# First norm's squares on ScalarE, the bias copy in eight requests, and idle products before the first chunk: one change to a hybrid decoder layer on Trainium2

## The chip, the core and the metric

The kernel runs on one core of one Trainium2 chip. The metric is the device time of one launch in microseconds (us); lower is better. The core has TensorE (PE, with its weight loads in a row of their own, PEld), VectorE (DVE), ScalarE (ACT), GpSimd (POOL), SyncE (SP), and sixteen DMA engines that all queues share. All inputs and outputs are in device memory.

## The reference, cut to what matters

One decoder layer is computed for a prompt of 256 tokens and for eight samples of four tokens (288 token columns in all, D = 2048), with the same weights:

```
mod = silu(c) @ w_ada + b_ada                 # 9 condition rows, 2048 x 12288 weights
shift1, scale1, gate1, shift2, scale2, gate2 = split(mod, 6)
h = rmsnorm(x, norm1_g) * (1 + scale1) + shift1
qa, ka, va, qb, kb, vb, r, glr = split(h @ w_in)
oa = dilated attention(qa, ka, va, rel_bias)  # 16 heads, prompt and samples
ob = gated linear attention(qb, kb, vb, gates from glr)   # 4 heads
x = x + gate1 * (concat(norm(oa), norm(ob) * silu(r)) @ w_out)
h2 = rmsnorm(x, norm2_g) * (1 + scale2) + shift2
x = x + gate2 * conv_ffn(h2)                  # w_up 2048 x 11264, w_down 5632 x 2048
```

`rmsnorm(x, g)` is `x * rsqrt(mean(x*x) + EPS) * g`, in float32. The prompt's attention adds to each score a bias that depends on the distance of query and key alone; it comes from a table of 32 buckets per head.

## The kernel before, in words

Everything is float32. A large product is made of three passes on TensorE with weights and activations split in an upper and a lower part (`three`, L903 to L905). Weights come in slabs of 1 MB into a ring of four slots; ScalarE makes the upper part of a chunk (L1418, 128 x 1024), VectorE the lower part (L1920), and TensorE multiplies: 24 matmuls a chunk. The 96 chunks of `w_in` are numbered j; a loop over j on every engine sets the order by hand, and the work of the other stages is woven into it at fixed numbers: slabs of `w_ada` (four matmuls, each in a quarter of the array, L853), the four heads of the linear attention (`head`, j from 28 on, eight apart) and the eight pairs of attention heads (`pair`, j from 63 on, four apart). Then follow the samples' attention, the output projection, the second norm and the two halves of the FFN.

The places that the change touches:

- **Start.** TensorE first runs six products that nobody reads (L796, 128 x 256), then turns x from rows of tokens to columns (`x_turns`, L818, 48 transposes), together with the condition rows and some vectors. VectorE copies each turned tile to `xT` (L1765).
- **First norm.** ScalarE squares `xT` in four pieces of 128 x 1152 (`norm_square`, L1367). TensorE sums each piece over the partitions by a product with ones (`norm_sum`, L839), which puts the sum of a token into all 128 partitions; a piece is woven between two slabs of `w_ada` (`early_slab`, L853). VectorE makes the mean (L1827), ScalarE takes logarithm and exponential (L1377, L1379), each after a load of its table, and VectorE multiplies `xT` by the root (`norm_rooted`, L1841).
- **Condition.** Slabs 0 to 7 of `w_ada` give the first group of shift and scale. After slab 3 and after slab 7 ScalarE copies the result rows (`ada_rows`, L1437), TensorE turns them (`early_turn`, L860, with nine columns), VectorE adds the bias (L1822), and modulates (L1897 to L1905). Only then can the first chunk be multiplied.
- **Bias.** A table of 16 x 512 is written to `bias_rows` in device memory (L699). One request (L706) copies it to `bias_full`, [16 heads, 128, 256], each row shifted by one element against the row before: 2048 pieces of 1 KB, device memory to device memory. GpSimd waits for it at once, and loads the first states of the linear attention (L715) after that. In the stage of the pairs, GpSimd loads the bias of each pair of heads from `bias_full` (L732, 256 KB). Its loop over the pairs is a hardware loop of four rounds.
- **Queues.** SP issues the slabs of `w_in` and the first ones of `w_ada` (L517, L539), ACT the later ones of `w_ada` (`lead_load`, L1455, and `late_load`, L1462); each waits until a slot is free. What GpSimd issues stands in a queue of its own.

Of the kernel before, what the change touches and what calls it, by code (L numbers as in the profile page):

```python
# [14 lines left out]
P = 128  # L15
# [119 lines left out]
def build(nc, a, o, bias_rows, bias_full):  # L135
    ctx = ExitStack()
    with ctx:
# [65 lines left out]
        rel_rows = projf[:, 11328:11456]  # L203
        sq = projf[:, 11520:13824].rearrange("p (j n c) -> p j n c", j=2, n=4)
        sq2 = [work[:, t:t + 2 * TOK].rearrange("p (n c) -> p n c", n=2) for t in (0, 944)]
# [32 lines left out]
        def old_state(b):  # L238
# [80 lines left out]
        PA_ = st("prep_scalar", "silu_c")  # L319
        NT = [st("norm1_tensor", "s0", "s1", "s2", "s3"), st("norm2_tensor", *(f"s{n}" for n in range(8)))]  # L320
        NA = [st("norm1_scalar", "q0", "q1", "q2", "q3", "ln", "rs"),
              st("norm2_scalar", *(f"q{n}" for n in range(8)), "ln", "rs")]
        NM = [st(f"norm{n}_mean", "ms") for n in (1, 2)]

# [186 lines left out]
        def _(sp):  # L511
            def ada_load(s):

                i, at = s // 8, 512 * (s // 8) + D * (s // 4 % 2)
                place, slot, _ = ada_home(s)
                dst = slab(slot, 4, 512) if place == 0 else (first_rows, lead_rows)[place - 1][slot]
                sp.dma_start(dst, w_ada[:, 4 * (s % 4):4 * (s % 4) + 4, at:at + 512]  # L517
                             ).then_inc((full, first_in, lead_in)[place][slot], 16)
# [57 lines left out]
            for s in range(2):  # L576
                sp.wait_ge(raw_used, s + 3)
                ada_load(s + 8)
            sp.wait_ge(*PT_.upto("x15"))
            ada_load(10)  # L580
            sp.wait_ge(*NT[0].upto("s3"))
            ada_load(11)
# [95 lines left out]
        def _(pool):  # L678
# [25 lines left out]
            pool.dma_start(wg2, a["w_gate2"][0]).then_inc(wg2_in, 16)  # L704
            slant = bass.AP(bias_rows[:, :].tensor, P - 1, [[512, H_A], [-1, P], [1, SEQ]])
            pool.dma_start(bias_full[:, :, :], slant).then_inc(slant_out, 16)  # L706
            pool.wait_ge(slant_out, 16)

            s_in = a["state_gla"][0].rearrange("(s e) h k v -> k h e s v", e=2)
            s_out = o["new_gla_s"].rearrange("(s e) h k v -> k h e s v", e=2)  # L710
            for h in range(H_B):
                if h:
                    pool.wait_ge(s0_out, 32 * h)
                for e in range(2):
                    pool.dma_start(s0[:, :, e, :], s_in[:, h, e]).then_inc(s0_in, 16)  # L715
                pool.wait_ge(*RA.upto("stp", h))
                pool.dma_start(o["new_gla_p"][h], stp).then_inc(stp_out, 16)
                pool.wait_ge(*RV.upto("state1", h))
                for e in range(2):
                    pool.dma_start(s_out[:, h, e], s0[:, :, e, :]).then_inc(s0_out, 16)  # L720

            pool.wait_ge(*RN.upto("o1", H_B - 1))
            by_head = bias_full[:, :, :].rearrange("h p c -> p h c")
            with pool.Fori(0, PAIRS // 2) as i:
                for j in range(2):
# [5 lines left out]
                    pool.sem_inc(pool_turns, 1)  # L731
                    pool.dma_start(bias_p[:, j], by_head[:, bass.ds(p * 2, 2), :]).then_inc(biasp_in[j], 16)  # L732
                    pool.wait_ge(*TV.upto("krows", p))
# [53 lines left out]
        def _(pe):  # L787
# [6 lines left out]
            pe.wait_ge(con_in, 16)  # L794
            for n in range(6):
                mm(ps[:, 7, 0:256], ident, con[:, 0:256], start=True, stop=True)  # L796

            def condition_turns():
# [33 lines left out]

            def norm_sum(j):

                pe.wait_ge(*NA[0].upto(f"q{j}"))
                if j == 0:
                    pe.wait_ge(*PV_.upto("vectors"))
                for k in range(4):
                    last = mm(ps[:, 4, 0:TOK], ones, sq[:, j % 2, k, :], start=(j + k == 0),  # L839
                              stop=(j == 3 and k == 3))  # L840
                last.then_inc(*NT[0].step(f"s{j}"))

# [29 lines left out]
            def early_turn(i, half):  # L872
                pe.wait_ge(*AA.upto("rows_b" if half else "rows_a", i))
                if half == 0:
                    pe.wait_ge(*AV.upto("mod", i - 1))
                ada_turn(6 if half else 5).then_inc(*AT.step("turn_b" if half else "turn_a"))

            for k in range(8):
# [475 lines left out]
        def _(act):  # L1354
# [7 lines left out]

            def norm_square(j):
                act.wait_ge(*PV_.upto(f"x{4 * j + 3}"))
                if j >= 2:
                    act.wait_ge(*NT[0].upto(f"s{j - 2}"))
                f(sq[:, j % 2], xT[:, 4 * j:4 * j + 4, :], ACT.Square).then_inc(*NA[0].step(f"q{j}"))  # L1367

# [5 lines left out]

            def norm_root(n):
                act.wait_ge(*NM[n].upto("ms"))
                f(rs, rs, ACT.Ln).then_inc(*NA[n].step("ln"))  # L1377
                act.wait_ge(*NA[n].upto("ln"))
                f(rs, rs, ACT.Exp, scale=-0.5).then_inc(*NA[n].step("rs"))  # L1379

# [57 lines left out]

            for j in range(4):
                norm_square(j)  # L1440
            ada_rows(0, 0)
            norm_root(0)
            ada_rows(0, 1)
# [217 lines left out]
            act.wait_ge(stp_out, 64)  # L1661
            norm_root(1)
            late_rows(13)
# [93 lines left out]
        def _(dve):  # L1757
            v = nc.vector
            for s_ in (PV_, *NM, *NG, *NS_, NP, *NL, CV, AV, BV, TQ, TV, TO, SQ, SV, SK[1], RV, RN, RG, OV, UV, NX, FV, FZ, DV_):
                dve.sem_inc(s_.sem, len(s_.names))  # L1760
            v.memset(c32[:, :, :], 0.0).then_inc(fill_c, 1)
            dve.wait_ge(fill_c, 1)
            def x_copy(k):
# [60 lines left out]

            def norm_mean(n, bank):
                dve.wait_ge(*NT[n].upto("s7" if n else "s3"))
                v.tensor_scalar(rs, ps[:, bank, 0:TOK], 1 / D, EPS, ALU.mult, ALU.add).then_inc(*NM[n].step("ms"))  # L1827

# [8 lines left out]
            def norm_rooted(j):  # L1837

                r = rs.rearrange("p (a c) -> p a c", a=1).to_broadcast([P, 4, TOK])
                dve.wait_ge(*NA[0].upto("rs"))  # L1840
                v.tensor_tensor(hraw[:, 4 * j:4 * j + 4, :], xT[:, 4 * j:4 * j + 4, :], r,  # L1841
                                ALU.mult).then_inc(*NP.step(f"t{j}"))
# [90 lines left out]
            rel_copies()  # L1933
            norm_mean(0, 4)
            biases()
# [351 lines left out]
            for j in range(5, 32 + LEAD):  # L2287
# [8 lines left out]
                if j == 13:  # L2296
                    late_mod(12)
            norm_mean(1, 4)
            dve.wait_ge(*NX.upto("x7"))
# [167 lines left out]
```

## Time and profile before

| | us |
|---|---|
| median of three runs | 1690.75 (1686.88 to 1693.04) |
| the profiled execution | 1691.79 |
| its span | 1690.2 |
| TensorE busy | 1629.7 (96%) |
| VectorE busy | 889.8 (53%) |
| ScalarE busy | 718.1 (42%) |
| GpSimd busy | 77.2 (5%) |
| mean granted clock of TensorE | 0.982 of full |
| DMA, mean over the span | 221 GB/s |

The span is what lies between the first and the last recorded instruction; the 1.6 us around it are the launch. The busy time of an engine is an average over stages with different limits. The chain of waits, followed back from the last instruction, is TensorE's for 90% of the span, so what matters is where TensorE waits, what it does that could be left out, and at which clock it runs.

### The profile page before, as it was taken

The numbers are of one execution on the slowest core, as the hardware profiler recorded it, in microseconds if no ns is written. First come the engines' busy times: TensorE is split into PE (matmuls) and PEld (weight loads), VectorE is DVE, ScalarE is ACT, GpSimd is POOL, SyncE is SP. The second block draws the span as 40 slices with busy tenths as digits, with TensorE's granted clock in tenths as the row PEclk, the third lists the DMA queues.
The fourth block names the chain that finished last, engine by engine and source line by source line (L and its number), as shares of the span: only waits on it lengthen the run. The fifth ranks groups of instructions, "written<-read, shape, count | busy, mean of one in ns | idle before, by whom it ended". The sixth has DMA issues, their size and how long they took to land.

```text
span 1690.2 us, 29353 instructions
## 1 busy us (share of the span) xinstructions
PE 1629.7 (96%) x12222; PEld 1459.2 (86%) x12222; DVE 889.8 (53%) x1555; ACT 718.1 (42%) x1018; POOL 77.2 (5%) x135
## 2 busy tenths in 40 slices
PE   8899899999999888999899999999999999999997
PEld 4678688788888543898799999999999999999996
DVE  2555354555566543654745545454455456656563
ACT  2332345445555433533533334333333345545452
POOL 2000000001111000000000000000000000000000
PEclk8999999999999998999999999999999999999999
DMA  9998867779778899575844454455454545555550
GB/s 334 368 372 282 284 231 269 242 270 311 264 247 282 314 353 375 182 246 160 290 150 152 161 180 161 152 177 166 160 161 152 175 143 175 183 165 169 161 186 15
DMA packets 276369, 372.80 MB, mean 221 GB/s; under 512 B 8097, under 2 KB 192771, under 8 KB 276233
## 3 DMA queue, kind: packets, MB, share of 16 engines
q1 hardware_dynamic: 232592, 279.62, 49.9%
q10 hardware_dynamic: 35922, 71.38, 11.9%
q0 software_dynamic: 7728, 19.97, 3.7%
q8 instruction: 97, 1.59, 0.4%
q14 instruction: 30, 0.25, 0.0%
HBM read 361.06 MB, written 11.97 MB: 221 GB/s over the span
## 4 chain that ended last, share of the span: by engine, by line
PE 90%; DVE 3%; DMA 3%; ACT 2%; issue 1%; SPq 1%; POOL 0%; ACTq 0%; DVEq 0%; POOLq 0%
PE ps L903 25%; PE ps L904 24%; PE ps L905 24%; PE ps L853 5%; DMA ring<-in_w_ada 2%; PE ps L1150 2%; PE ps L860 1%; PE ps L1165 1%; PE ps L1195 1%; DMA ring<-in_cache_k_win 1%; PE ps L818 1%; DVE wlo L1920 1%; PE ps L839 1%; PE ps L847 0%; PE ps L1079 0%
## 5 line engine op out<-in xcount | busy, mean ns | idle before, releaser
L903 PE MATMUL ps<-hhi,whi 128*128 128x288 f32 x3136 | 942.3, 300 | 11.0 <-DVE hlo L1887 5.7
L905 PE MATMUL ps<-hhi,wlo 128*128 128x288 f32 x3136 | 926.5, 295 | 0.0
L904 PE MATMUL ps<-hlo,whi 128*128 128x288 f32 x3136 | 926.4, 295 | 0.0
L903 PEld LDWEIGHTS ps<-hhi,whi 128*128 128x128 f32 x3136 | 591.1, 188 | 49.7 <-issue 40.8
L904 PEld LDWEIGHTS ps<-hlo,whi 128*128 128x128 f32 x3136 | 590.6, 188 | 0.9
L905 PEld LDWEIGHTS ps<-hhi,wlo 128*128 128x128 f32 x3136 | 591.0, 188 | 0.0
L1795 DVE TENSOR_TENSOR wlo<-ring,whi 128x1024 fp32r<-128x1024 f32 x178 | 212.1, 1221 | 92.4 <-ACT whi L1401 91.9
L1401 ACT ACTIVATE whi<-ring 128x1024 fp32r<-128x1024 f32 x178 | 184.4, 1057 | 161.9 <-PE ps L905 161.9
L1920 DVE TENSOR_TENSOR wlo<-ring,whi 128x1024 fp32r<-128x1024 f32 x96 | 117.2, 1223 | 124.7 <-ACT whi L1418 124.5
L1418 ACT ACTIVATE whi<-ring 128x1024 fp32r<-128x1024 f32 x96 | 100.8, 1052 | 133.5 <-PE ps L905 112.9
L2408 DVE TENSOR_TENSOR wlo<-ring,whi 128x1024 fp32r<-128x1024 f32 (+1 forms) x94 | 105.6, 1130 | 57.3 <-ACT whi L1727 57.3
L1727 ACT ACTIVATE whi<-ring 128x1024 fp32r<-128x1024 f32 (+1 forms) x94 | 91.8, 981 | 75.0 <-PE ps L905 75.0
L2322 DVE TENSOR_TENSOR hlo<-proj,hhi 128x1152 fp32r<-128x1152 f32 (+3 forms) x56 | 60.9, 1099 | 48.3 <-ACT hhi L1674 47.5
L853 PE MATMUL ps<-ring,c 128*32 128x512 f32 x544 | 70.1, 626 | 8.9 <-DMA ring<-in_w_ada 8.9
L1674 ACT ACTIVATE hhi<-proj 128x1152 fp32r<-128x1152 f32 (+3 forms) x56 | 52.7, 955 | 50.7 <-PE ps L905 50.6
L2343 DVE TENSOR_SCALAR work<-work,small 128x304 f32<-128x304 f32 x44 | 17.3, 436 | 100.0 <-ACT work L1686 100.0
L2355 DVE TENSOR_TENSOR proj<-ps,work 128x512 f32<-128x512 f32 x22 | 15.2, 692 | 85.6 <-PE ps L905 85.6
L1685 ACT ACTIVATE work<-ps 128x512 f32<-128x512 f32 x22 | 13.2, 598 | 110.6 <-PE ps L905 110.6
L1150 PEld LDWEIGHTS ps<-con,ring 128*128 128x128 f32 x320 | 36.9, 147 | 24.1 <-issue 13.7
L1150 PE MATMUL ps<-con,ring 128*128 128x128 f32 x320 | 45.4, 291 | 9.1 <-DVE kcT L2182 4.3
L1409 ACT ACTIVATE whi<-ring 128x1024 fp32r<-128x1024 f32 x32 | 33.2, 1054 | 48.1 <-PE ps L905 32.0
L1802 DVE TENSOR_TENSOR wlo<-ring,whi 128x1024 fp32r<-128x1024 f32 x32 | 38.2, 1219 | 16.4 <-ACT whi L1409 16.2
(297 smaller groups left out, 1177.2 us busy)
## 6 DMA issues: line engine op xcount, KB each, us to landing
ring<-in_w_up SPq DMA_DIRECT2D x88, 1024.0 KB, 5.1
ring<-in_w_ada ACTq DMA_DIRECT2D x58, 1024.0 KB, 8.2
ring<-in_w_in SPq DMA_DIRECT2D x48, 1024.0 KB, 9.0
ring<-in_w_down SPq DMA_DIRECT2D x32, 1408.0 KB, 6.7
ring<-in_cache_k_win SPq DMA_DIRECT2D x16, 1024.0 KB, 11.7
ring<-in_w_out SPq DMA_DIRECT2D x16, 1024.0 KB, 5.9
proj<-in_w_ada SPq DMA_DIRECT2D x14, 1024.0 KB, 10.1
vals<-in_cache_v_win SPq DMA_DIRECT2D x12, 1024.0 KB, 10.3
```

The lines of the kernel that those rows point to most:

```text
L853: last = mm(ps[32 * k:32 * k + 32, bank, :], c32[:, 4 * (s % 4) + k, :], rows[:, k, :], start=(s % 4 == 0), stop=(s % 4 == 3))
L903: mm(out, w_hi, x_hi, start=start, stop=False)
L904: mm(out, w_hi, x_lo, start=False, stop=False)
L905: return mm(out, w_lo, x_hi, start=False, stop=stop)
L1150: last = turn(ps[:, 2 * (n % 2) + t // 4, P * (t % 4):P * (t % 4) + P], slab(u, KT, 512)[:, t, P * m:P * m + P], ident)
L1401: f(whi[:, j % BUFS, 0:n], ring[:, s % SLOTS, n * (j % 2):n * (j % 2) + n], ACT.Copy).then_inc(hi_done, 1)
L1418: f(whi[:, j % BUFS, :].rearrange("p (k c) -> p k c", k=4), in_chunk_of(rows, j), ACT.Copy).then_inc(hi_done, 1)
L1727: f(whi[:, jj % BUFS, 0:n], ring[:, s % SLOTS, CHUNK * kc:CHUNK * kc + n], ACT.Copy).then_inc(hi_done, 1)
L1795: v.tensor_tensor(wlo[:, j % BUFS, 0:n], ring[:, s % SLOTS, n * (j % 2):n * (j % 2) + n], whi[:, j % BUFS, 0:n].bitcast(F32), ALU.subtract ...
L1920: v.tensor_tensor(wlo[:, j % BUFS, :].rearrange("p (k c) -> p k c", k=4), in_chunk_of(rows, j), whi[:, j % BUFS, :].bitcast(F32).rearrange ...
L2322: last = v.tensor_tensor(hlo[:, at:at + m, :], actT[:, k0:k0 + m, :], hhi[:, at:at + m, :].bitcast(F32), ALU.subtract)
L2408: v.tensor_tensor(wlo[:, jj % BUFS, 0:n], ring[:, (2 * kg + h) % SLOTS, CHUNK * kc:CHUNK * kc + n], whi[:, jj % BUFS, 0:n].bitcast(F32), A ...
```

## The change

Four things are changed.

1. The squares of the first norm are taken from x's rows. ScalarE squares each half row of each of three tiles of tokens (six activations, 128 x 1024 or 32 x 1024) and gives the sum over the row beside it. VectorE adds the two halves, divides and adds EPS; ScalarE takes logarithm and exponential of 128 x 3 numbers; VectorE spreads them on the diagonal of three matrices (`diag`), and three products of ones with these (128, 128 and 32 columns) put each token's root into all partitions. VectorE copies that to `rs`. The four groups of four products with ones are gone.
2. TensorE's order at the start is another: slabs 0 to 3, the three products, slab 4, the biases, the first turn, slabs 5 to 7, the second turn. SP's loads of slabs 10 and 11 wait for the new steps.
3. Behind the second turn stand sixteen products that nobody reads (128 x 256, into bank 7). The first six now write bank 6.
4. The copy of `bias_rows` to `bias_full` is eight requests of two heads each (256 KB). The first two are issued after the stores of the states of heads 2 and 3 of the linear attention; the others in the loop over the pairs, the request for pair p + 2 behind the load of the bias of pair p. GpSimd waits for piece p just ahead of that load. The loop is written out.

```
-            slant = bass.AP(bias_rows[:, :].tensor, P - 1, [[512, H_A], [-1, P], [1, SEQ]])
-            pool.dma_start(bias_full[:, :, :], slant).then_inc(slant_out, 16)
-            pool.wait_ge(slant_out, 16)
+            def slant(p):
+                rows = bass.AP(bias_rows[:, :].tensor, 1024 * p + P - 1, [[512, 2], [-1, P], [1, SEQ]])
+                pool.dma_start(bias_full[2 * p:2 * p + 2, :, :], rows).then_inc(slant_out, 16)
...
                     pool.dma_start(s_out[:, h, e], s0[:, :, e, :]).then_inc(s0_out, 16)
+                if h >= 2:
+                    slant(h - 2)
...
-            with pool.Fori(0, PAIRS // 2) as i:
+            for i in range(PAIRS // 2):
...
+                    pool.wait_ge(slant_out, 16 * (p + 1))
+                    pool.dma_start(bias_p[:, j], by_head[:, 2 * p:2 * p + 2, :]).then_inc(biasp_in[j], 16)
+                    if p + 2 < PAIRS:
+                        slant(p + 2)
...
+            def norm_roots():
+
+                pe.wait_ge(*NM[0].upto("diag"))
+                pe.wait_ge(*PV_.upto("vectors"))
+                for t in range(3):
+                    n = P if t < 2 else NS
+                    last = mm(ps[:, 4, P * t:P * t + n], ones[0:n, :], diag[0:n, t, 0:n], start=True, stop=True)
+                last.then_inc(*NT[0].step("roots"))
+
+            def idle_products(bank, n):
+
+                for _ in range(n):
+                    mm(ps[:, bank, 0:256], ident, con[:, 0:256], start=True, stop=True)
...
-            early_slab(0)
-            early_slab(1)
-            norm_sum(0)
-            early_slab(2)
-            norm_sum(1)
-            early_slab(3)
-            norm_sum(2)
+            for s in range(4):
+                early_slab(s)
+            norm_roots()
             early_slab(4)
-            norm_sum(3)
-            early_slab(5)
             biases()
             early_turn(0, 0)
-            early_slab(6)
-            early_slab(7)
+            for s in range(5, 8):
+                early_slab(s)
             early_turn(0, 1)
+            idle_products(7, 16)
...
+            def norm_squares():
+
+                act.wait_ge(*NM[0].upto("zero"))
+                for n in range(2):
+                    act.wait_ge(x_in[n], 32)
+                    for t in range(3):
+                        m, q = P if t < 2 else NS, 3 * n + t
+                        if q:
+                            act.wait_ge(*NA[0].upto(f"q{q - 1}"))
+                        f(x_squares[0:m], xr[0:m, t, D // 2 * n:D // 2 * n + D // 2], ACT.Square,
+                          accum_out=x_sums[0:m, 2 * t + n:2 * t + n + 1]).then_inc(*NA[0].step(f"q{q}"))
...
+            def norm_roots():
+
+                dve.wait_ge(*NA[0].upto("q5"))
+                halves_of = x_sums.rearrange("p (t n) -> p t n", n=2)
+                v.tensor_tensor(roots, halves_of[:, :, 0], halves_of[:, :, 1], ALU.add).then_inc(*NM[0].step("sum"))
+                dve.wait_ge(*NM[0].upto("sum"))
+                v.tensor_scalar(roots, roots, 1 / D, EPS, ALU.mult, ALU.add).then_inc(*NM[0].step("ms"))
+                dve.wait_ge(*NA[0].upto("rs"))
+                for t in range(3):
+                    last = v.tensor_scalar(diag[:, t, :], ident, roots[:, t:t + 1], None, ALU.mult)
+                last.then_inc(*NM[0].step("diag"))
+                dve.wait_ge(*NT[0].upto("roots"))
+                v.tensor_copy(rs, ps[:, 4, 0:TOK]).then_inc(*NM[0].step("rs"))
```

TensorE's order from slab 0 (L853 before, L864 now) to the first product of the first chunk (L903, L910). The operands name the place: `ring,c` and `vals,c` are slabs, `proj,con` the first norm, `con,mrow` the turns. Before:

```order
L853 MATMUL ps<-ring,c 32x512 x8
L839 MATMUL ps<-proj,con 128x288 x4
L853 MATMUL ps<-ring,c 32x512 x4
L839 MATMUL ps<-proj,con 128x288 x4
L853 MATMUL ps<-ring,c 32x512 x4
L839 MATMUL ps<-proj,con 128x288 x4
L853 MATMUL ps<-vals,c 32x512 x4
L839 MATMUL ps<-proj,con 128x288 x4
L853 MATMUL ps<-vals,c 32x512 x4
L826 MATMUL ps<-proj 16x512
L829 MATMUL ps<-proj 128x512
L830 MATMUL ps<-proj 128x160
```

And with the change, as far as the first product:

```order
L864 MATMUL ps<-ring,c 32x512 x16
L846 MATMUL ps<-proj,con 128x128 x2
L846 MATMUL ps<-proj,con 128x32
L864 MATMUL ps<-vals,c 32x512 x4
L833 MATMUL ps<-proj 16x512
L836 MATMUL ps<-proj 128x512
L837 MATMUL ps<-proj 128x160
L871 MATMUL ps<-con,mrow 128x9 x4
L864 MATMUL ps<-vals,c 32x512 x12
L871 MATMUL ps<-con,mrow 128x9 x4
L852 MATMUL ps<-con 128x256 x16
L910 MATMUL ps<-hhi,whi 128x288
```

The sixteen products with ones are three smaller ones, slab 5 has moved behind the first turn, and sixteen idle products stand between the second turn and the first chunk.

GpSimd's queue before, from the weights of the gates to the first stores of a state (`bias_slant_out` counts the copy of the bias):

```order
L704 DMA qkS<-in_w_gate 16x512 [waits prep_split_vector]
L706 DMA bias_full<-bias_rows 2048x1x256
L715 DMA ring<-in_state_gla 128x4x256 [waits bias_slant_out]
L715 DMA ring<-in_state_gla 128x4x256
L717 DMA out_new_gla_p<-proj 128x256 [waits gla_scalar]
```

And with the change, the same place and then the end of the heads and the first pair:

```order
L708 DMA qkS<-in_w_gate 16x512 [waits prep_split_vector]
L720 DMA ring<-in_state_gla 128x4x256 x2
L722 DMA out_new_gla_p<-proj 128x256 [waits gla_scalar]
...
L725 DMA out_new_gla_s<-ring 128x4x256
L712 DMA bias_full<-bias_rows 256x1x256
L740 DMA work<-bias_full 128x2x256 [waits gla_output,pair_squares,bias_slant_out]
L712 DMA bias_full<-bias_rows 256x1x256
L748 DMA out_new_k_p<-kv_rows 128x2x128 [waits pair_vector]
L749 DMA out_new_k_s<-proj 32x128
```

The copy and the wait for it have left the place ahead of the first states; an eighth of the copy stands behind the last stores of a head, and another behind each load of a pair's bias.

## Rows read from the trace of the kernel before

**Rows 1.** The page's chain of waits: shares of the span by engine

```profile
PE 90%; DVE 3%; DMA 3%; ACT 2%; issue 1%; SPq 1%; POOL 0%; ACTq 0%; DVEq 0%; POOLq 0%
```

**Rows 2.** Windows: PE, PEld, DVE, ACT, POOL busy (instructions), clock, DMA share, GB/s

```profile
48.00:55.00 7.00, 3.67 (x16) 3.70 (x17) 6.97 (x14) 4.29 (x7) 0.00 (x0) 0.52 0.95 335
60.00:100.00 40.00, 40.00 (x306) 30.46 (x304) 18.60 (x32) 14.49 (x24) 0.00 (x0) 1.00 1.04 378
```

**Rows 3.** Timeline of the start: start, us, engine, line, operation [idle before]

```profile
4.79 5.49 PE L796 MATMUL ps<-con 128*128 128x256 f32 x12 [4.79 <-DMA con<-in_tables]
...
25.09 1.59 DVE L1777 COPY proj<-proj 32x8 f32<-32x8 f32 x16
...
27.73 2.21 PE L839 MATMUL ps<-proj,con 128*128 128x288 f32 x8
...
34.84 1.28 ACT L1377 ACT_TABLE_LOAD   x1
...
43.34 1.92 PE L853 MATMUL ps<-vals,c 128*32 128x512 f32 x16
...
46.08 1.03 PE L860 MATMUL ps<-con,mrow 128*128 128x9 f32 x8 [0.81 <-ACT mrow L1437]
...
51.33 0.58 PE L903 MATMUL ps<-hhi,whi 128*128 128x288 f32 x1 [4.22 <-DVE hlo L1912]
...
56.24 1.07 PE L853 MATMUL ps<-ring,c 128*32 128x512 f32 x8
```

**Rows 4.** Slabs 6 and 7 of `w_ada`: issues and time to landing

```profile
L517 SPq DMA_DIRECT2D vals<-in_w_ada x2: 1129/1856/2584, 18.8 to 21.4; - x2
...
DMA to landing us min/median/max: 18.3/18.4/18.4
```

**Rows 5.** Slabs 16 and 17 of `w_ada`: issues, landing, and their use

```profile
L1455 ACTq DMA_DIRECT2D ring<-in_w_ada x2: 374/713/1052, 72.2 to 73.0; - x2
...
DMA to landing us min/median/max: 10.9/11.9/12.8
...
85.83 1.92 PE L853 MATMUL ps<-ring,c 128*32 128x512 f32 x16
```

**Rows 6.** The bias copy's issue, in the answer on its tile

```profile
L706 POOL DMA_DIRECT2D bias_full<-bias_rows x1: 1035/1035/1035, 154.9 to 154.9; - x1
```

**Rows 7.** DMA from 157 to 166 us: packets, MB, share; time to landing

```profile
q0 software_dynamic: 441, 1.80, 101.4%
q10 hardware_dynamic: 14, 0.03, 1.7%
...
ring<-in_w_ada ACTq DMA_DIRECT2D x2, 1024.0 KB, 19.4
```

**Rows 8.** Timeline of TensorE behind the copy: slabs 34 and 35

```profile
176.50 1.07 PE L853 MATMUL ps<-ring,c 128*32 128x512 f32 x8
183.75 1.94 PE L853 MATMUL ps<-ring,c 128*32 128x512 f32 x8 [6.19 <-DMA ring<-in_w_ada]
```

**Rows 9.** Windows as in 2, behind the wait, and of the pairs' stage

```profile
183.70:188.00 4.30, 4.25 (x18) 2.58 (x19) 0.00 (x0) 0.60 (x1) 0.00 (x0) 0.51 0.96 299
...
390.00:560.00 170.00, 167.48 (x1262) 140.15 (x1261) 101.66 (x246) 94.89 (x159) 26.11 (x41) 1.00 0.79 268
```

**Rows 10.** Two slabs behind the third head's stores: issues, landing, and use

```profile
L1462 ACTq DMA_DIRECT2D ring<-in_w_ada x2: 374/374/374, 333.6 to 334.5; - x2
...
DMA to landing us min/median/max: 11.5/12.6/13.6
...
348.60 1.92 PE L853 MATMUL ps<-ring,c 128*32 128x512 f32 x16
```

**Rows 11.** The first pair's bias: its load, the page's landing, its first use

```profile
393.61 0.72 POOL L732 DMA_DIRECT2D work<-bias_full  x1 [11.95 <-DVE proj L2085]
...
work<-bias_full POOLq DMA_DIRECT2D x8, 256.0 KB, 4.4
...
406.48 0.27 DVE L2109 SCALAR_TENSOR_TENSOR proj<-ps,work 128x128 f32<-128x128 f32 x1
```

More of the change, by code:

```diff
@@ L203, in build @@
         rel_rows = projf[:, 11328:11456]
-        sq = projf[:, 11520:13824].rearrange("p (j n c) -> p j n c", j=2, n=4)
+        x_squares = projf[:, 11520:12544]
+        diag = projf[:, 12544:12928].rearrange("p (t c) -> p t c", t=3)
+        x_sums, roots = projf[:, 12928:12934], projf[:, 12936:12939]
         sq2 = [work[:, t:t + 2 * TOK].rearrange("p (n c) -> p n c", n=2) for t in (0, 944)]
@@ L319, in build @@
         PA_ = st("prep_scalar", "silu_c")
-        NT = [st("norm1_tensor", "s0", "s1", "s2", "s3"), st("norm2_tensor", *(f"s{n}" for n in range(8)))]
-        NA = [st("norm1_scalar", "q0", "q1", "q2", "q3", "ln", "rs"),
+        NT = [st("norm1_tensor", "roots"), st("norm2_tensor", *(f"s{n}" for n in range(8)))]
+        NA = [st("norm1_scalar", *(f"q{n}" for n in range(6)), "ln", "rs"),
               st("norm2_scalar", *(f"q{n}" for n in range(8)), "ln", "rs")]
-        NM = [st(f"norm{n}_mean", "ms") for n in (1, 2)]
+        NM = [st("norm1_mean", "zero", "sum", "ms", "diag", "rs"), st("norm2_mean", "ms")]
         NX = st("norm2_scaled", *(f"x{n}" for n in range(8)))
@@ L579, in _ @@
             sp.wait_ge(*PT_.upto("x15"))
+            sp.wait_ge(*NA[0].upto("q5"))
             ada_load(10)
-            sp.wait_ge(*NT[0].upto("s3"))
+            sp.wait_ge(*NT[0].upto("roots"))
+            sp.wait_ge(*NM[0].upto("diag"))
             ada_load(11)
@@ L794, in _ @@
             pe.wait_ge(con_in, 16)
-            for n in range(6):
-                mm(ps[:, 7, 0:256], ident, con[:, 0:256], start=True, stop=True)
             def condition_turns():
@@ L831, in biases @@
                    stop=True).then_inc(*PT_.step("bias_s"))
[L833 to L841, printed above, removed]
+            def norm_roots():
[8 more added lines that the diff above has]
+                    mm(ps[:, bank, 0:256], ident, con[:, 0:256], start=True, stop=True)
             def norm2_sum(n):
@@ L876, in early_turn @@
                 ada_turn(6 if half else 5).then_inc(*AT.step("turn_b" if half else "turn_a"))
+            idle_products(6, 6)
             for k in range(8):
@@ L1373, in norm2_square, with root @@
                 f(sq2[n % 2], xT[:, 2 * n:2 * n + 2, :], ACT.Square).then_inc(*NA[1].step(f"q{n}"))
-            def norm_root(n):
+            def root(n, r):
                 act.wait_ge(*NM[n].upto("ms"))
-                f(rs, rs, ACT.Ln).then_inc(*NA[n].step("ln"))
+                f(r, r, ACT.Ln).then_inc(*NA[n].step("ln"))
                 act.wait_ge(*NA[n].upto("ln"))
-                f(rs, rs, ACT.Exp, scale=-0.5).then_inc(*NA[n].step("rs"))
+                f(r, r, ACT.Exp, scale=-0.5).then_inc(*NA[n].step("rs"))
             def norm_hi(j):
@@ L1437, in ada_rows @@
                 f(mrow[:, :], ps[:, 7 if half else 3, :], ACT.Copy).then_inc(*AA.step("rows_b" if half else "rows_a"))
-            for j in range(4):
-                norm_square(j)
+            norm_squares()
+            root(0, roots)
             ada_rows(0, 0)
-            norm_root(0)
             ada_rows(0, 1)
@@ L1661, in _ @@
             act.wait_ge(stp_out, 64)
-            norm_root(1)
+            root(1, rs)
             late_rows(13)
@@ L1761, in _ @@
             v.memset(c32[:, :, :], 0.0).then_inc(fill_c, 1)
+            v.memset(x_sums, 0.0).then_inc(*NM[0].step("zero"))
             dve.wait_ge(fill_c, 1)
@@ L1823, in mod, with norm2_mean @@
                 last.then_inc(*AV.step("mod"))
-            def norm_mean(n, bank):
-                dve.wait_ge(*NT[n].upto("s7" if n else "s3"))
-                v.tensor_scalar(rs, ps[:, bank, 0:TOK], 1 / D, EPS, ALU.mult, ALU.add).then_inc(*NM[n].step("ms"))
+            def norm_roots():
[10 more added lines that the diff above has]
+                v.tensor_copy(rs, ps[:, 4, 0:TOK]).then_inc(*NM[0].step("rs"))
+            def norm2_mean():
+                dve.wait_ge(*NT[1].upto("s7"))
+                v.tensor_scalar(rs, ps[:, 4, 0:TOK], 1 / D, EPS, ALU.mult, ALU.add).then_inc(*NM[1].step("ms"))
             def norm_scale(n, k0, m):
@@ L1839, in norm_rooted @@
                 r = rs.rearrange("p (a c) -> p a c", a=1).to_broadcast([P, 4, TOK])
-                dve.wait_ge(*NA[0].upto("rs"))
+                dve.wait_ge(*NM[0].upto("rs"))
                 v.tensor_tensor(hraw[:, 4 * j:4 * j + 4, :], xT[:, 4 * j:4 * j + 4, :], r,
@@ L1933, in _ @@
             rel_copies()
-            norm_mean(0, 4)
+            norm_roots()
             biases()
@@ L2297, in _ @@
                     late_mod(12)
-            norm_mean(1, 4)
+            norm2_mean()
             dve.wait_ge(*NX.upto("x7"))
```

6 lines of the change are left out of this document (removed).

## The prediction, made before the changed kernel was run

> **What bounds the kernel now.** I read the chain of waits first: TensorE carries 90% of the span [rows 1], so time can only be won where TensorE waits, runs slowly, or does work that nobody needs. The windows name two such places in reach of this change. From 48 to 55 us TensorE is busy for 3.67 of 7 us at half clock (0.52); from 60 us on it works without a gap, 306 instructions in 40 us or 0.13 us each [rows 2]. The second is a wait of 6.19 us at 183.75 [rows 8], with a stretch at 0.51 of the clock behind it [rows 9].
>
> In the timeline of the start [rows 3] the reader should see what holds the first chunk: slabs 6 and 7 of the condition (ending at 45.26), ScalarE's copy, the turn (46.08 to 47.11), VectorE's modulation, and only at 51.33 the first product. From the end of the last slab to the first product it is 6.1 us. The slabs landed earlier than they were used: slab 7 was issued at 21.4 and took 18.4 us, so it lay there at 39.8 [rows 4]. TensorE was late because of the four groups of sums (2.21 us each, 8.8 in all).
>
> The wait at 183.75 has its cause in another queue. The bias copy was issued at 154.9 [rows 6]. From 157 to 166 us its queue has 1.80 MB and all of the DMA time (101.4%); the queue of ScalarE, which had issued two slabs at about 160, gets 1.7%, and these slabs need 19.4 us to land [rows 7]. TensorE uses the first at 176.50, and stands still for the second until 183.75 [rows 8].
>
> **The change part by part.** All of it is set against the profiled execution, 1691.8 us.
>
> *Start.* With the 8.8 us of sums gone, slab 7's landing at 39.8 is what TensorE waits for. Is all else in time? VectorE ends its small copies at 26.68 [rows 3]; then come two small steps, two table loads of 1.28 us [rows 3], two activations and three diagonals, by rows of that size some 0.3 us each: about 31 us. TensorE's three products of 288 columns together (a quarter of a group of sums, 0.6), slab 4 (half of the 1.92 at 43.34), the biases (1184 columns at the pace of the sums, 2.3), the turn (1.0), slabs 5 and 6 (2.0) end at about 38, before 39.8; at half clock they would end at about 45, and this cover would be gone. ScalarE's six squares of about 1.1 us are done by 18 us, beside the turning of x. The new steps cost nothing as long as slab 7 is later.
>
> Then: slab 7 until 40.9, turn until 42.7. Without idle products the first chunk could start 6.1 us after the slab, at 47.0. But sixteen products stand ahead of it. Their price at full clock is 2.21 / 4 x 256 / 288 = 0.49 us each, 7.9 us in all; cold, six took 5.49 [rows 3], 0.92 each, 14.6 us. So the first chunk starts at 50.6 with a warm engine and ends 24 x 0.13 = 3.1 us later, at 53.7; before, it started at 51.33, partly at half clock, and slab 8 followed at 56.24 [rows 3]. That is 2.5 us won. With all sixteen cold it is 57.3 + 3.1 = 60.4, 4.2 us lost. A mixture is nearest: after 51.33 the clock was back by about 55, for the mean up to there is 0.52 and from 60 on 1.00 [rows 2]. So a cold start would make four of the sixteen cost 0.43 us more, and the gain would be 0.8.
>
> A second limit: at 60 to 100 us the DMA engines are at 1.04 [rows 2], as full as they get. Slab 17 was issued at 73.0, landed at 85.8, and is the second half of the work that starts at 85.83, needed at 86.8 [rows 5]: 1.0 us to spare. TensorE can be ahead by that and by the 0.7 us that the DMA engines had free at 48 to 55 us ((1.05 - 0.95) x 7, rows 2), so by 1.7 us. The term lies between 0.8 and 1.7 of gain, **-1.2**; its ends are -1.7 and +4.2.
>
> The rule of the Trainium skill that bears on the idle products is in "TensorE: Matmul & The Clock Gate", section "Why this matters for your kernels": leave no idle gaps between bursts of matmuls, or the clock falls to half. The trace agrees that it fell while TensorE waited for the first chunk (0.52, rows 2). Taken alone the rule would give the warm case, the end at -1.7, and a sum lower by 0.5 us; it doesn't count the 7.9 us that the products themselves take in a gap of 4.2.
>
> *The bias copy.* Without it the DMA engines have, from 155 to 177 us, the first states (1 MB, now issued at once and not after the copy), the two slabs, and two slabs of `w_in`: 5.2 MB, at the 378 GB/s of rows 2 some 14 us if all came at once; with the states gone before 160 it is 11 us from 160, so 171, and slab 35 is needed at 177.6. The wait goes: 6.19 us. The slab behind it took 1.94 us at half clock against 1.07 for its twin [rows 8]: 0.9. Behind that the clock was half until about 188 [rows 9], 2.3 us of products that take half as long at full clock: 1.1. Term: **-8.2**. Next in line there is the chunk's slab of `w_in`, which in the same 11 us lands as well.
>
> *The pieces.* An eighth of the copy takes 9 / 1.80 x 0.26 = 1.3 us of all DMA engines [rows 7]. Piece 0 comes behind the stores of the third head, at about 335, with two slabs in flight: these were issued at 333.6 and 334.5, the later one landed 13.6 us on, at 348.1, and is needed at 349.6 [rows 10]. 1.5 us to spare against 1.3. The others fall into the heads' end and the pairs' stage, where the DMA engines are at 0.79 and TensorE idles 2.5 of 170 us [rows 9]; six pieces add 7.9 us to 36 free ones. GpSimd's queue: each piece is issued behind the bias of a pair, ahead of the stores of the keys, for which GpSimd waits some 12 us anyway. The load of the bias itself waits for a piece issued two pairs earlier, and has 12.9 us from issue to first use for a landing of 4.4 [rows 11]. The bounds are 0 and 8 x 1.3 = 10.4; nearest is rows 10, so I take **+0.3**.
>
> The hardware loop written out, the memset and the shifted loads of slabs 10 and 11 are hidden: SP's queue is full of earlier slabs at that time. The first six products only change bank.
>
> Sum: -1.2 - 8.2 + 0.3 = -9.1, or 1682.7 against the profiled 1691.8. The median shown is 1.0 lower than that execution, and against it the same sum gives **1681.7 us**, which is my forecast.
>
> **The rivals.**
>
> *The wait is only halved.* The copy may not be all of it: four large requests still start within a microsecond of 160. For it speaks that slabs took 11 to 13 us under full load [rows 5]; 160.5 + 13 is 173.5, though, still before 177.6. If slab 35 came at 181, 3.4 us of wait and the cold clock would remain: 4.4 us less gained, 1686.1.
>
> *The idle products run cold.* The clock may have fallen while TensorE waited for slab 7. All sixteen at 0.92 us: +4.2 in place of -1.2, 1687.1.
>
> *All ends good:* the DMA limit gives way and the warm start counts in full, 2.5 us, and the pieces cost nothing: 1680.1.
>
> *Slower: the pieces starve the slabs.* In rows 7 a copy from device memory to device memory held all engines while others waited. If each of the eight pieces delays what is in flight not by its 1.3 us but by the 4.4 us that a request of its size takes to land [rows 11], then, with 1.5 us to spare [rows 10], TensorE waits 2.9 us eight times: 23.2 - 9.4 = +13.8, 1704.6. It decides from 3.7 us of delay a piece on ((9.4 + 8.5) / 8 + 1.5). Against it speaks the free fifth of the DMA time in that stage [rows 9]. The Trainium skill's page "DMA: Bandwidth & Descriptors", section "Anatomy of one DMA — SWDGE (gpsimd) path", speaks for small requests being dear: about 2 us fixed and bytes over 436 GB/s. By it, as an estimate, a piece takes 2.6 us, and all eight in TensorE's path would make +11.5, 1702. No run here shows such a piece yet; the 4.4 us of rows 11 is more than the page's figure.
>
> **How the numbers follow.** A measurement of this kernel can tell about 0.5%, 8.5 us, from no change. Chances: the forecast 0.54, the halved wait 0.15, cold products 0.13, all good 0.13, starved slabs 0.05. The three runs of before lie 6 us apart, so each case is blurred by 2 to 3 us. The bound of faster is 1682.3; of the forecast's own chance a little over half lies under it, of the good case most, of the two weaker ones a sixth: faster 0.46. Slower has 0.04 of its case; the rest, 0.50, is within 0.5%. The range takes 1677.5 (all good, less the blur) to 1688.5 (the weaker two and a blur of 1.5); outside lie the starved slabs and the tails.
>
> **What would show it.** Right: slab 7 used at its landing near 40 us; the first chunk's products from about 50.6 at full clock; no wait for a slab of `w_ada` between 160 and 200 us and no half clock there; pieces that land within 5 us each; about 9 us less up to 200 us, and the same distances from there to the end. Wrong: TensorE still late at slab 7 (roots too late), sixteen products taking over 12 us, waits for slabs at 85 to 95 us that give the start's gain back by more than 1 us, a wait at slab 35 of several microseconds, or new waits for slabs or the bias at 335 to 560 us.

## The result, and the profile after

The changed kernel takes 1694.34 us (median, 1692.78 to 1699.22) against 1690.75 before (1686.88 to 1693.04): the ratio is 1.0026, with a 95% interval of [1.0015, 1.0038]. Both medians are of seven runs. It is slower by a quarter of a percent, where 9 us less had been forecast. The profiled execution took 1692.78 us, with a span of 1690.9.

The two terms of the forecast can be found in the profile, and so can a loss that it had put at 0.3 us. First the place of the old wait. From 170 to 190 us TensorE is busy all the time, and at full clock (the columns are those of rows 2):

```profile
170.00:190.00 20.00, 20.00 (x154) 16.24 (x153) 9.27 (x19) 5.23 (x6) 0.00 (x0) 1.00 0.60 197
```

These are some of TensorE's slabs of `w_ada` (L864 now), and the idle products (L852), in the timeline of the changed kernel from the start to 476 us (start, us, engine, line, operation, and the idle time before it; one slab is eight recorded matmuls, a pair of slabs sixteen):

```profile
37.00 4.08 PE L864 MATMUL ps<-vals,c 128*32 128x512 f32 x24
42.79 7.15 PE L852 MATMUL ps<-con 128*128 128x256 f32 x32
53.07 1.06 PE L864 MATMUL ps<-ring,c 128*32 128x512 f32 x8
...
175.35 1.92 PE L864 MATMUL ps<-ring,c 128*32 128x512 f32 x16
187.89 1.92 PE L864 MATMUL ps<-ring,c 128*32 128x512 f32 x16
...
322.77 1.92 PE L864 MATMUL ps<-ring,c 128*32 128x512 f32 x16
338.88 1.07 PE L864 MATMUL ps<-ring,c 128*32 128x512 f32 x8
342.70 1.24 PE L864 MATMUL ps<-ring,c 128*32 128x512 f32 x8 [2.75 <-DMA ring<-in_w_ada]
...
392.98 1.06 PE L864 MATMUL ps<-ring,c 128*32 128x512 f32 x8
397.57 1.49 PE L864 MATMUL ps<-ring,c 128*32 128x512 f32 x8 [3.52 <-DMA ring<-in_w_ada]
...
458.64 1.92 PE L864 MATMUL ps<-ring,c 128*32 128x512 f32 x16
472.75 1.06 PE L864 MATMUL ps<-ring,c 128*32 128x512 f32 x8
475.09 1.07 PE L864 MATMUL ps<-ring,c 128*32 128x512 f32 x8 [1.27 <-DMA ring<-in_w_ada]
```

And the same slabs in the kernel before:

```profile
197.31 1.92 PE L853 MATMUL ps<-ring,c 128*32 128x512 f32 x16
...
332.49 1.92 PE L853 MATMUL ps<-ring,c 128*32 128x512 f32 x16
...
397.79 1.92 PE L853 MATMUL ps<-ring,c 128*32 128x512 f32 x16
...
458.19 1.92 PE L853 MATMUL ps<-ring,c 128*32 128x512 f32 x16
472.30 1.93 PE L853 MATMUL ps<-ring,c 128*32 128x512 f32 x16
```

Slabs 34 and 35 stand together at 175.35; before, the first came at 176.50 and the second at 183.75 [rows 8]. The next pair is at 187.89 and was at 197.31: 9.4 us earlier. The pair of slabs at 322.77 stood at 332.49: the changed kernel is 9.7 us ahead at this point. The next pair [rows 10] is torn apart: its second half, at some 349.5 before (half of the 1.92 us behind 348.60), waits until 342.7, so only 6.8 us are left. The one at 392.98 comes with 4.8 us of lead (397.79 before), its second half with 1.1, and at 458.64 the changed kernel is 0.5 us behind. At 472.75 a third pair is torn apart. The whole lead was given back inside 140 us.

The waits of TensorE between 325 and 480 us say for what:

```profile
PE ps L864 <- DMA ring<-in_w_ada: 7.5, 3, 3.5
```

Three waits for a slab, 7.5 us in all (total, times, longest). The kernel before has none in this stretch. The windows of the first two places show that the clock fell too (the columns are those of rows 2):

```profile
338.00:347.00 9.00, 6.25 (x37) 4.16 (x36) 3.53 (x10) 3.47 (x10) 0.00 (x0) 0.81 1.03 353
390.00:402.00 12.00, 8.48 (x53) 6.14 (x53) 4.24 (x7) 5.28 (x6) 1.04 (x1) 0.86 0.84 261
```

What stands in the way? The answer on the tile of the copy shows when the pieces are issued, and who is said to wait for one of them:

```profile
L712 POOL DMA_DIRECT2D bias_full<-bias_rows x8: 1102/1108/1117, 325.2 to 498.4; - x8
...
  POOL work L740: 11.1, 1
```

The answer on the line of the pieces, for the first one alone:

```profile
L712 POOL DMA_DIRECT2D bias_full<-bias_rows x1: 1106/1106/1106, 325.2 to 325.2; - x1
...
DMA to landing us min/median/max: 15.9/15.9/15.9
```

The first piece of 256 KB needs 15.9 us to land; over all eight it is 9.2 to 15.9, with a median of 11.9. The first is as long on its way as the whole copy of 2 MB was before (the DMA issues of the kernel before from 150 to 160 us: number, size and landing):

```profile
bias_full<-bias_rows POOLq DMA_DIRECT2D x1, 2048.0 KB, 15.6
```

What is in flight beside the pieces is late. The two slabs torn apart at 392.98 were issued at 380.6 and 381.5 and landed after 11.8 and 16.0 us; before, the same two needed 5.5 and 9.1. The 11.1 us of GpSimd, though, are not lost to a piece: by the code this load waits for the first piece alone, which had landed at 341, and GpSimd stood 11.95 us at the same place before, for VectorE [rows 11]. And the page's list of queues holds a hint. This is GpSimd's queue in the changed kernel (packets, MB, share):

```profile
q0 software_dynamic: 11424, 20.02, 3.6%
```

And in the kernel before:

```profile
q0 software_dynamic: 7728, 19.97, 3.7%
```

3696 packets more, for the same data and 0.05 MB. The page counts them all as under 512 bytes. Seven requests more account for 7 x 16 = 112 packets of completion, so 3584 are left, 448 for each of the eight pieces. 448 is 14 x 32. The Trainium skill states a rule that fits, on the page "DMA: Bandwidth & Descriptors". Its section "Why a DMA increments its semaphore by 16 and not by 1" says that a request runs on the largest number of engines up to 16 that divides the slowest dimension of its two sides, and "Rules for kernel authors" says to keep a multiple of 16 there. The slowest dimension of the old request was 16 heads; that of a piece is 2. By this rule a piece runs on two of the sixteen DMA engines, and the other fourteen would get 32 fillers each. The trace has no engine numbers; that the count comes out as 14 x 32 agrees with the rule.

### The profile page after: what moved, and what is told of

Its sections match the earlier page's. It is cut to its first block, busy times and chain, and to the rows that moved or that the text cites. A ratio compares the mean times of both kernels' runs of the same rounds, so it can differ in the third digit from the quotient of the medians.

```text
span 1690.9 us, 29291 instructions
## 1 busy us (share of the span) xinstructions
PE 1630.1 (96%) x12228; PEld 1460.2 (86%) x12228; DVE 890.9 (53%) x1561; ACT 720.3 (43%) x1026; POOL 85.3 (5%) x142
## 2 busy tenths in 40 slices
DMA packets 280065, 372.86 MB, mean 221 GB/s; under 512 B 11793, under 2 KB 196467, under 8 KB 279929
## 4 chain that ended last, share of the span: by engine, by line
PE 83%; DMA 8%; DVE 4%; ACT 2%; issue 1%; SPq 1%; POOL 0%; ACTq 0%; DVEq 0%; POOLq 0%
PE ps L910 24%; PE ps L911 23%; PE ps L912 23%; PE ps L864 4%; DMA ring<-in_w_ada 4%; DMA ring<-in_w_in 2%; PE ps L1157 2%; DMA proj<-in_w_ada 1%; PE ps L871 1%; DVE wlo L1947 1%; PE ps L1172 1%; PE ps L1202 1%; DMA ring<-in_cache_k_win 1%; ACT whi L1431 1%; DMA proj<-in_tables 0%
## 5 line engine op out<-in xcount | busy, mean ns | idle before, releaser
L910 PE MATMUL ps<-hhi,whi 128*128 128x288 f32 x3136 | 942.4, 301 | 6.8 <-DVE hlo L1914 5.7
L910 PEld LDWEIGHTS ps<-hhi,whi 128*128 128x128 f32 x3136 | 591.1, 188 | 45.2 <-issue 36.7
L864 PE MATMUL ps<-ring,c 128*32 128x512 f32 x544 | 69.4, 620 | 10.3 <-DMA ring<-in_w_ada 10.3
L2370 DVE TENSOR_SCALAR work<-work,small 128x304 f32<-128x304 f32 x44 | 17.3, 436 | 100.6 <-ACT work L1698 100.6
L1815 DVE TENSOR_TENSOR wlo<-ring,whi 128x1024 fp32r<-128x1024 f32 x32 | 38.2, 1221 | 16.1 <-ACT whi L1422 15.9
## 6 DMA issues: line engine op xcount, KB each, us to landing
vals<-in_cache_v_win SPq DMA_DIRECT2D x12, 1024.0 KB, 10.1
```

Source lines behind the costliest of these rows:

```text
L864: last = mm(ps[32 * k:32 * k + 32, bank, :], c32[:, 4 * (s % 4) + k, :], rows[:, k, :], start=(s % 4 == 0), stop=(s % 4 == 3))
L910: mm(out, w_hi, x_hi, start=start, stop=False)
```

## The experiments

Two theories stood against each other: a piece holds up what is in flight because it runs on **few engines**, so that the share of every other request on these engines is late; or any copy of this size does so at **a bad time**. Each ratio is against runs of the kernel before on the same chip, with a median of 1690.88 us for the first four experiments below and of 1691.75 for the other four.

**The start alone.** The changed kernel with the bias copy as before:

```
-                rows = bass.AP(bias_rows[:, :].tensor, 1024 * p + P - 1, [[512, 2], [-1, P], [1, SEQ]])
-                pool.dma_start(bias_full[2 * p:2 * p + 2, :, :], rows).then_inc(slant_out, 16)
+            slant = bass.AP(bias_rows[:, :].tensor, P - 1, [[512, H_A], [-1, P], [1, SEQ]])
+            pool.dma_start(bias_full[:, :, :], slant).then_inc(slant_out, 16)
+            pool.wait_ge(slant_out, 16)
...
```

> The new first norm, TensorE's new order and the sixteen idle products, with the bias copy as one request at its old place. Both theories of the loss (few DMA engines per piece; bytes at a bad time) say that the start has no part in it: slab 8 some 3 us earlier than before, 1.1 to 1.5 us left of that from slab 18 on, the wait for slab 35 there as before (about 6 to 7 us), and a median 1 to 2 us below that of before. If the start were the cause of the loss, it would be at or above before.

Measured: 1690.82 us, ratio 0.9999 [0.9986, 1.0011]. The wait for slab 35 is there (total, times and longest, from 150 to 560 us):

```profile
PE ps L858 <- DMA ring<-in_w_ada: 6.1, 2, 5.8
```

The start is not the cause of the loss, as both theories have it. But no gain shows either, where 1 to 2 us were expected; the interval, from -2.4 to +1.9 us, would also hold a gain of that size. In the profile the first product came at 52.16 and slab 8 only 0.6 us earlier than before. TensorE had waited 2.64 us for slab 4, and behind that the clock was at half (0.50 from 36 to 42 us): slabs 5 to 7 took 5.01 us, and 4.08 in the changed kernel.

**The pieces alone.** The kernel before with the eight pieces, their places and waits:

```
+                if h >= 2:
+                    slant(h - 2)
...
+                    pool.wait_ge(slant_out, 16 * (p + 1))
...
+                    if p + 2 < PAIRS:
+                        slant(p + 2)
```

Measured: 1696.44 us, ratio 1.0026 [1.0013, 1.0039]. That is inside the 3 to 6 us above before that were expected. The lead is 7.4 us at 221.6 (before: 229.0), and at 478.51 the kernel is 6.2 us behind (before: 472.30):

```profile
221.58 1.93 PE L859 MATMUL ps<-ring,c 128*32 128x512 f32 x16
...
478.51 1.07 PE L859 MATMUL ps<-ring,c 128*32 128x512 f32 x8
480.01 1.06 PE L859 MATMUL ps<-ring,c 128*32 128x512 f32 x8 [0.43 <-DMA ring<-in_w_ada]
```

So the pieces make the whole loss, and more than all that they win.

**Twins: two engines or sixteen.** Both issue two pieces of 256 KB behind the stores of each of the four heads, and wait for all eight ahead of the first pair. They differ in the pattern alone. The first has two heads and 128 rows to a piece:

```
-                if h >= 2:
-                    slant(h - 2)
+                slant(2 * h)
+                slant(2 * h + 1)
...
-                    pool.wait_ge(slant_out, 16 * (p + 1))
+                    pool.wait_ge(slant_out, 128)
...
-                    if p + 2 < PAIRS:
-                        slant(p + 2)
```

> The changed kernel with two pieces of two heads each behind the stores of every one of the four heads; all eight are waited for ahead of the first pair. Few engines: each piece again lands in 10 us or more, slabs of w_ada in flight beside it land 4 to 8 us later than in the twin run with all sixteen heads per piece, and TensorE waits several times for them between 230 and 390 us, 6 to 15 us in all; 3584 small packets. Bytes at a bad time: the same as the twin within 1.5 us.

Its twin has sixteen heads and 16 rows to a piece:

```
-                rows = bass.AP(bias_rows[:, :].tensor, 1024 * p + P - 1, [[512, 2], [-1, P], [1, SEQ]])
-                pool.dma_start(bias_full[2 * p:2 * p + 2, :, :], rows).then_inc(slant_out, 16)
+                rows = bass.AP(bias_rows[:, :].tensor, P - 1 - 16 * p, [[512, H_A], [-1, 16], [1, SEQ]])
+                pool.dma_start(bias_full[:, 16 * p:16 * p + 16, :], rows).then_inc(slant_out, 16)
```

> Its twin: the same places and bytes, but each piece is sixteen rows of all sixteen heads, so that the slowest dimension of the request is 16 and not 2. Few engines: no small packets beyond those of before, a piece lands in 4 to 6 us, no wait for a slab over 1.5 us between 150 and 550 us, and a median of 1681 to 1684, about 10 us below the changed kernel. Bytes at a bad time: the same waits as its twin, 1690 or more.

Measured: 1709.85 us with two heads (ratio 1.0107 [1.0084, 1.0129]), 1688.41 with sixteen (0.9988 [0.9972, 1.0004]). The same bytes, issued at the same places: 21.4 us apart. In the profiles slab 40 starts at 219.94 and 219.87, slab 62 at 428.77 and 404.26, so 24.5 us of the 24.8 between the profiled executions are made where the pieces are in flight. This parts the theories. The waits for slabs (L862) and for `w_in` (L1429) from 190 to 420 us in the two-head kernel:

```profile
ACT whi L1429 <- DMA ring<-in_w_in: 26.7, 6, 7.5
...
PE ps L862 <- DMA ring<-in_w_ada: 8.1, 4, 3.0
```

And in its twin:

```profile
ACT whi L1429 <- DMA ring<-in_w_in: 13.8, 4, 4.7
...
PE ps L862 <- DMA ring<-in_w_ada: 0.2, 1, 0.2
```

The pieces among the DMA issues of the same stretch, of the two-head kernel and then of its twin:

```profile
bias_full<-bias_rows POOLq DMA_DIRECT2D x8, 256.0 KB, 13.4
```

```profile
bias_full<-bias_rows POOLq DMA_DIRECT2D x8, 256.0 KB, 7.5
```

And GpSimd's queue on their pages, in the same order:

```profile
q0 software_dynamic: 11424, 20.02, 3.4%
```

```profile
q0 software_dynamic: 7840, 19.97, 3.4%
```

7840 packets are 7728 and the 112 of seven more completions: no filler is left. One thing more differs between the twins: a piece writes two blocks of 128 KB in the one and sixteen of 16 KB in the other. No run keeps the blocks and changes the engines alone; that it is the engines rests on the rule of the Trainium skill, the counts of fillers and the landing times. The products' waits for slabs in this stretch are 0.2 us and no longer 8.1, ScalarE's for `w_in` half as long. But the twin falls short of the 1681 to 1684 expected. A piece lands in 7.5 us (median; 5.5 to 11.6) and not in 4 to 6, and the lead shrinks from 9.2 us at slab 40 to 6.9 at slab 70, so bytes at a bad time are worth some 2 us. Another 2 us of lead go between 534 and 658 us, long after the last piece, and the twelve runs scatter from 1682.7 to 1696.2; the rest of the gap is not settled.

**Four engines.** Four requests of four heads each, one behind the stores of each head:

```
+                rows = bass.AP(bias_rows[:, :].tensor, 2048 * p + P - 1, [[512, 4], [-1, P], [1, SEQ]])
+                pool.dma_start(bias_full[4 * p:4 * p + 4, :, :], rows).then_inc(slant_out, 16)
```

> Four requests of four heads, one behind the stores of each head: the same bytes and places as the runs with two pieces per head, and a slowest dimension of 4. 
Measured: 1706.49 us, ratio 1.0086 [1.0071, 1.01]. Its requests among the DMA issues from 190 to 420 us:

```profile
bias_full<-bias_rows POOLq DMA_DIRECT2D x4, 512.0 KB, 13.2
```

And GpSimd's queue on its page:

```profile
q0 software_dynamic: 9312, 19.99, 3.4%
```

The fillers fit again, with twelve engines that get no data: 9312 - 7728 - 3 x 16 = 1536 = 4 x 12 x 32. The time lies between the two relatives, but outside the range expected, near the end of two engines. By the rule of the Trainium skill, twice the engines with requests of twice the size leave each engine the same load per request, 128 KB, and the landing is the same 13 us. The whole copy puts 128 KB on each of sixteen engines and needs 15.6; a piece of the twin with sixteen heads puts 16 KB on each and needs 7.5. So the landing follows what one engine gets at once.

**One request, early.** The changed kernel with the copy as one request of sixteen heads, when slab 30 has been used, which nobody waits for until the first pair:

```
+            pool.wait_ge(raw_used, 31)
+            slant = bass.AP(bias_rows[:, :].tensor, P - 1, [[512, H_A], [-1, P], [1, SEQ]])
+            pool.dma_start(bias_full[:, :, :], slant).then_inc(slant_out, 16)
             pool.wait_ge(*CV.upto("glr_lo"))
...
+            pool.wait_ge(slant_out, 16)
             by_head = bias_full[:, :, :].rearrange("h p c -> p h c")
...
```

> The changed kernel with the bias copy as one request of all sixteen heads, issued at about 143 us when slab 30 has been used, and nobody waiting for it until the first pair. If the loss came from pieces on two DMA engines, nothing of it is left: no wait for a slab at 183 us and none over 1 us up to 550 us, TensorE 8 to 10 us ahead of before from 200 us to the end, a median of 1681 to 1684. If any copy at all costs the 8 us somewhere, the wait appears at another slab between 145 and 250 us and the median is 1688 or more.

Measured: 1682.06 us, ratio 0.9942 [0.9928, 0.9956]. The median is as expected. Slabs 34 and 35 stand together, as do all later pairs up to 560 us, and at slab 70 TensorE is 8.5 us ahead (463.80 against 472.30):

```profile
176.49 1.92 PE L859 MATMUL ps<-ring,c 128*32 128x512 f32 x16
...
463.80 1.92 PE L859 MATMUL ps<-ring,c 128*32 128x512 f32 x16
```

A copy of 2 MB that takes 15.5 us to land again costs nothing here: from 146 to 157 us the DMA engines of the kernel before have time left, half of it in the mean (the last but one column is their share):

```profile
146.00:150.00 4.00, 4.00 (x32) 3.00 (x31) 2.05 (x3) 1.85 (x3) 0.00 (x0) 1.00 0.47 175
150.00:154.00 4.00, 4.00 (x33) 4.00 (x33) 2.32 (x5) 1.06 (x1) 0.00 (x0) 1.00 0.81 265
154.00:157.00 3.00, 3.00 (x25) 3.00 (x24) 2.83 (x11) 0.94 (x3) 1.54 (x2) 1.00 0.12 41
```

**The same without the sixteen idle products.**

```
-            idle_products(7, 16)
```

> The same without the sixteen idle products. If they only fill a gap, the first chunk starts at the same time, at half clock, and the median is 1 to 2 us higher. If they stand in the way, as 7.9 us in a gap of about 4, the first product comes 2 to 5 us earlier, partly at half clock, and slab 8 is 0 to 2 us earlier; the median within 1 us of the run with them.

Measured: 1681.04 us, ratio 0.994 [0.9927, 0.9953], about 1 us from the run with them, which is less than those runs lie apart. The timeline without them:

```profile
44.26 1.03 PE L866 MATMUL ps<-con,mrow 128*128 128x9 f32 x8 [0.82 <-ACT mrow L1444]
49.52 0.58 PE L904 MATMUL ps<-hhi,whi 128*128 128x288 f32 x1 [4.23 <-DVE hlo L1933]
54.28 1.07 PE L859 MATMUL ps<-ring,c 128*32 128x512 f32 x8
```

And with them (the run before this one):

```profile
41.83 1.85 PE L866 MATMUL ps<-con,mrow 128*128 128x9 f32 x8 [0.81 <-ACT mrow L1445]
43.53 9.59 PE L847 MATMUL ps<-con 128*128 128x256 f32 x32
```

Without them the gap is 4.2 us, and the first chunk runs at half clock in part (0.73 from 50 to 55 us). With them the gap is filled by 9.59 us of products, since the clock was at half when they began (0.50 from 42 to 46 us), and the first real product comes at 52.76, 3.2 us later than without.

**The kernel before with the early request alone.** The same edit on the kernel before.

> The kernel before with nothing but the copy's single request moved to about 143 us and its wait to the first pair. The term of 8.2 us alone: the wait of 6.19 us gone, the clock full at 185 us, and a median 7 to 9 us below before, 1682 to 1684. The difference to the run with the new start, 0 to 1.5 us, is the start's whole worth.

Measured: 1681.3 us, ratio 0.9943 [0.993, 0.9956]:

```profile
156.87 1.92 PE L854 MATMUL ps<-ring,c 128*32 128x512 f32 x16
174.83 1.92 PE L854 MATMUL ps<-ring,c 128*32 128x512 f32 x16
...
462.21 1.92 PE L854 MATMUL ps<-ring,c 128*32 128x512 f32 x16
```

From slab 32 (158.53 before, 1.7 us earlier here) to slab 70 (472.30, 10.1 earlier) the lead grows by 8.4 us. The median is a little under the 1682 to 1684 expected. The 1.7 us that were there ahead of the copy come from a start whose code is that of before: slab 8 is at 54.57 here, at 56.24 in the profile of before and at 57.09 with the pieces alone, so single profiles of one start differ by 2.5 us. A few moved lines give all the gain that was measured; the new start adds nothing that can be told from this scatter.

## Why the prediction was wrong

- **The bias copy, -8.2: right.** The wait for slab 35 and the half clock behind it had their cause in the copy, and it was worth 8.2 us in the changed kernel (the lead grows from 1.2 at slab 34 to 9.4 at slab 36) and 8.4 in the last experiment. That several requests start at once was no obstacle; the rival of the halved wait is out.
- **The pieces, +0.3: this is the step that failed.** The prediction took an eighth of the copy as an eighth of its time, "1.3 us of all DMA engines", and so assumed that a piece spreads over sixteen engines as the whole had. By its pattern, and by the count of fillers, it doesn't. The same bytes in the same places with sixteen heads per piece cost 21.4 us less than with two. In the changed kernel the term was about 11 us (a lead of 9.7 at 323 us, 1.7 behind at slab 72, 490.92 against 489.22): 7.5 us of waits for slabs, and beside them the clock behind these waits and ScalarE's later slabs of `w_in` (14.8 us of waits from 190 to 420 us against 7.7). That is above the upper bound of 10.4, which had been built from the same eighth. The prediction had the case as its slower rival, "the pieces starve the slabs", with the right place (new waits for slabs from 335 us on), but a chance of 0.05. Its price per piece was the landing of an SBUF load of the same size, 4.4 us, and a wait of 2.9 us for each of eight; the pieces land in 9 to 16, and three pairs of slabs are torn apart. The free fifth of DMA time that spoke against it says little, because it is a mean over sixteen engines: it would look the same with two late and fourteen free.
- **The rule that was there.** The prediction weighed the fixed cost for small requests on the page "DMA: Bandwidth & Descriptors" of the Trainium skill, and overlooked, on the same page, the rule on the number of engines, which the order of the instructions already hinted at: `2048x1x256` had become `256x1x256`, with a slowest dimension of 2 in the code.
- **The start, -1.2.** In the changed kernel's profile it was -1.15 from slab 18 to slab 34. The forecast limit worked as described: slab 8 was 3.2 us early (53.07 against 56.24), and TensorE then waited three times for slabs up to 100 us, 1.7 us in all. But that was a lucky execution. In the five other profiles with the new start and the idle products slab 8 was 0.0 to 0.9 us early, and the median of the start alone shows nothing (0.9999). What the term left out is a wait for slab 4: the prediction let TensorE wait for slab 7 alone. It was 0.42 us in the changed kernel and 0.9 to 2.6 in the five others. In three of them slabs 5 to 7 then took 5.0 to 5.4 us at half clock; in the other two TensorE waited 1.7 us for slab 7, and the idle products began at half clock and took 9.6 to 9.9 us. The fear that the cover is gone at half clock was right: slabs 5 to 7 took 4.08 us from 37.00 on in the changed kernel as well, at a clock of 0.52:

```profile
33.00:40.00 7.00, 7.00 (x29) 3.67 (x32) 3.03 (x5) 0.00 (x0) 0.50 (x1) 0.52 1.05 389
```

- **The idle products.** The rule on gaps that the prediction took from the Trainium skill holds for the clock, which stays at full from 43 to 55 us in the changed kernel. They fill more than the gap, though: 7.15 us at full clock, near the 7.9 reckoned, and 9.59 partly at half, in place of 4.2. Leaving them out costs nothing that can be measured.

## What to carry to other kernels

When a request is cut into pieces, look at the slowest dimension of each side after the cut. By the rule of the Trainium skill's page "DMA: Bandwidth & Descriptors" a piece whose outermost count is 2 loads two DMA engines; here such pieces held up what was in flight, though the mean DMA share was 0.84 from 390 to 402 us. Here it was better to move the transfer whole to a stretch with free DMA time, and its wait to the first reader, than to cut it up; that alone was worth 0.57%. And a gain that a wait hides should be followed to the end of the span by the start of the same work in both timelines, not only past the place of the old wait. Single profiles of one start differ by 2.5 us here, so a gain of 1 us is not read from one of them.

## What the runs showed of the hardware that was not expected

- Requests of 256 KB from device memory to device memory with an outermost count of 2 land in 9.2 to 15.9 us (median 11.9) in the changed kernel and in 6.9 to 17.3 (13.4) in the two-head experiment, with a count of 16 in 7.5 (median); the whole 2 MB needs 15.6. An eighth of the bytes, by the rule of the Trainium skill on an eighth of the engines, takes nearly the time of the whole.
- The small packets come out as 32 for each engine that by the rule of the Trainium skill gets no data: 448 a request with two engines, 384 with four, none with sixteen. The page's count of packets under 512 bytes (8097 before, 11793 after) shows this without a look at any single transfer.
